# Layer 0's phase table built by GpSimd instead of VectorE, and the last input product of the state space in another PSUM bank

## The reference, cut to what matters

```
h = rmsnorm(x, norm_mix[l])
u, sq, sk, sv, dq, dk, dv, gate_logits = jnp.split(h @ w_in[l], split_idx, axis=-1)
y_ssm = jax.nn.gelu(s5_ssm(u, ...))            # the state space
y_sb  = stick_breaking_attention(sq, sk, sv)
o     = differential_attention(dq_r, dk_r, dv, lam)
...
lam_bar = jnp.exp(lam * dt)                    # in s5_ssm: one complex number for each of 2048 states
bu = jnp.einsum('gpc,blgc->blgp', b_bar, ug)
_, states = lax.associative_scan(_ssm_combine, (a, bu), axis=1)
```

## Time and profile before

| what | value |
|---|---|
| time, median of 3 runs | 1025.34 us (1024.87 to 1025.78) |
| time of the profiled execution | 1024.67 us |
| its span from the first to the last instruction | 1023.0 us |
| granted TensorE clock, mean | 0.997 of full speed |
| PE busy / DVE busy / ACT busy / POOL busy | 96% / 75% / 54% / 5% |

### The profile page before, as it was taken

How to read it: one execution, slowest core, us unless ns; L and a number is a source line. 1 busy time by engine, 2 the same in 40 slices (tenths; PEclk the granted TensorE clock), 3 DMA queues, 4 the chain that set the end, 5 groups by cost and what they waited for, 6 DMA issues and landing times. The chain is left out here.

```text
span 1023.0 us, 17644 instructions
## 1 busy us (share of the span) xinstructions
PE 985.5 (96%) x6784; PEld 872.3 (85%) x6784; DVE 764.5 (75%) x1185; ACT 549.9 (54%) x843; POOL 47.3 (5%) x104
## 2 busy tenths in 40 slices
PE   6999999999999999999999999999999999999996
PEld 6877889999897888888889778999988878888885
DVE  5988997878765866879765669887887567656665
ACT  7455426475755645544463663545656565444543
POOL 5004000000000004000000110000000000000000
PEclk9999999999999999999999999999999999999999
DMA  9797438466654666686657853565565546666652
GB/s 339 230 191 179 125 103 268 147 168 184 181 148 124 244 189 183 190 228 187 191 145 206 169 156 104 151 196 152 179 182 168 141 128 188 194 191 188 186 187 80
DMA packets 64164, 181.37 MB, mean 177 GB/s; under 512 B 19729, under 2 KB 21777, under 8 KB 63441
## 3 DMA queue, kind: packets, MB, share of 16 engines
q1 hardware_dynamic: 63648, 179.91, 60.3%
q10 hardware_dynamic: 432, 0.32, 0.1%
HBM read 176.67 MB, written 3.54 MB: 176 GB/s over the span
## 5 line engine op out<-in xcount | busy, mean ns | idle before, releaser
L1289 DVE TENSOR_TENSOR s_w_lo<-s_raw,s_w_hi 128x1024 fp32r<-128x1024 f32 x312 | 374.1, 1227 | 95.6 <-ACT s_w_hi L914 92.0
L914 ACT ACTIVATE s_w_hi<-s_raw 128x1024 fp32r<-128x1024 f32 x312 | 320.1, 1054 | 180.2 <-PE p_T L1877 78.2
L1875 PE MATMUL p_T<-s_hT,s_w_hi 128*128 128x256 f32 x576 | 166.4, 289 | 1.5 <-ACT s_w_hi L914 1.5
L1876 PE MATMUL p_T<-s_hT,s_w_hi 128*128 128x256 f32 x576 | 163.4, 284 | 0.0
L1877 PE MATMUL p_T<-s_hT,s_w_lo 128*128 128x256 f32 x576 | 163.2, 283 | 0.0
L1875 PE MATMUL p_A<-s_w_hi,s_bT_hi 128*128 128x512 f32 x320 | 125.1, 391 | 2.5 <-DVE s_bT_lo L1289 2.5
L1877 PE MATMUL p_A<-s_w_hi,s_bT_lo 128*128 128x512 f32 x320 | 124.8, 390 | 0.0
L1876 PE MATMUL p_A<-s_w_lo,s_bT_hi 128*128 128x512 f32 x320 | 124.6, 389 | 0.0
L1875 PEld LDWEIGHTS p_T<-s_hT,s_w_hi 128*128 128x128 f32 x576 | 110.8, 192 | 5.5 <-issue 2.7
L1876 PEld LDWEIGHTS p_T<-s_hT,s_w_hi 128*128 128x128 f32 x576 | 110.9, 193 | 0.1
L1877 PEld LDWEIGHTS p_T<-s_hT,s_w_lo 128*128 128x128 f32 x576 | 110.9, 192 | 0.0
(11 more groups left out here) (269 smaller groups left out, 1826.6 us busy)
## 6 DMA issues: line engine op xcount, KB each, us to landing
s_raw<-in_weights SPq DMA_DIRECT2D x312, 512.0 KB, 3.7
s_bt<-in_ssm_bt SPq DMA_DIRECT2D x2, 1024.0 KB, 7.4
s_gates<-f_turn SPq DMA_DIRECT2D x16, 128.0 KB, 7.6
s_x<-in_x SPq DMA_DIRECT2D x1, 1024.0 KB, 10.1
s_dv<-in_ssm_bc SPq DMA_DIRECT2D x2, 512.0 KB, 8.9
u_turn<-s_st_y SPq DMA_DIRECT2D x4, 256.0 KB, 4.9
s_uB<-u_turn SPq DMA_DIRECT2D x16, 64.0 KB, 5.1
s_bt<-in_mem SPq DMA_DIRECT2D x1, 1024.0 KB, 7.1
```

What stands on the lines that cost most here:

```text
L914: return nc.scalar.activation(o, i, f, **kw)
L1289: return V.tensor_tensor(o, i0, i1, op)
L1875: mm(o, lhi, rhi, start=first, stop=False, **kw)
L1876: mm(o, lhi, rlo, start=False, stop=False, **kw)
```

## The change

Two independent edits.

1. In layer 0 the phase table is made by POOL, all six steps in one go (`phases`), right after `tables`. The memsets and the 24 elementwise instructions are the same; the scratch is `dN[1]`, the buffer that dk will be evacuated to, so ACT's evacuation of dk waits for `phase_ready`. On DVE the calls of `p_ph` in layer 0 are gone. Layer 1's table stays on DVE.
2. `ssm_in` part 3 goes to bank A3 in place of A1, in both layers.

```diff
-                    ph=((6, 2, 2), (6, 3, 2), (7, 4, 2), (8, 5, 0), (9, 5, 1)), bt=(10, 11, 12)))
-        after(0, "p_ph0")
+                    bt=(10, 11, 12)))
...
-        [["A1", "A0", "A1", "A1"][s[1]]] if s[0] == "ssm_in" else
+        [["A1", "A0", "A1", "A3"][s[1]]] if s[0] == "ssm_in" else
...
+            def phases(st):
+
+                pool.wait_ge(*st.at(cs_ready, 1))
+                nc.gpsimd.memset(phase[:, 0, :, 0:1], 1.0).then_inc(*st.mid())
+                nc.gpsimd.memset(phase[:, 1, :, 0:1], 0.0).then_inc(*st.mid())
+                for k in range(TAB_STEPS):
+                    pool.wait_ge(*st.mine())
+                    c, e, o, q = phase_step(k, dN[1].rearrange("p t n -> p (t n)"))
+                    tt(o, e, c[0]).then_inc(*st.mid())
+                    tt(q, e, c[1]).then_inc(*st.mid())
+                    pool.wait_ge(*st.mine())
+                    tt(o[:, 0], o[:, 0], q[:, 1], ALU.subtract).then_inc(*st.mid())
+                    tt(o[:, 1], o[:, 1], q[:, 0], ALU.add).then_inc(*(st.sig(phase_ready) if k + 1 == TAB_STEPS else st.mid()))
...
                 if l == 0:
                     tables(st, 0)
+                    phases(st)
...
+                        if kind == "dk":
+                            act.wait_ge(*st.at(phase_ready, 1))
...
-                    elif kind == "p_ph0":
-                        for k in range(2):
-                            p_ph(0, k)
-                            dve.wait_ge(*st.mine())
```

More of the change, by code:

```diff
@@ L170, in pre @@
             after(u["bt"][n], "p_bt", tgt, n)
-        for at, k, part in u["ph"]:
-            after(at, "p_ph", tgt, k, part)
+        for at, k in u.get("ph", ()):
+            after(at, "p_ph", tgt, k)
     if l == 0:
         pre(0, dict(ct=-1, f=(2, 3), cv=(3, 4), b0=5,
-                    ph=((6, 2, 2), (6, 3, 2), (7, 4, 2), (8, 5, 0), (9, 5, 1)), bt=(10, 11, 12)))
-        after(0, "p_ph0")
+                    bt=(10, 11, 12)))
         after(6, "mm_k", 0)
@@ L185, in side_stages @@
         pre(1, dict(ct=up0 + 9, f=(up0 + 13, up0 + 13), cv=(up0 + 12, up0 + 13), b0=up0 + 16,
-                    ph=((up0 + 17, 0, 2), (up0 + 17, 1, 2), (up0 + 17, 2, 2), (up0 + 17, 3, 2),
-                                              (up0 + 20, 4, 2), (up0 + 21, 5, 2)), bt=(up0 + 24, up0 + 25, up0 + 28)))
+                    ph=((up0 + 17, 0), (up0 + 17, 1), (up0 + 17, 2), (up0 + 17, 3), (up0 + 20, 4), (up0 + 21, 5)),
+                    bt=(up0 + 24, up0 + 25, up0 + 28)))
     else:
@@ L468, in hybrid_trunk, with phase_step @@
         e_b = [gates[:, 2 * h:2 * h + 2, :] for h in range(XA_HEADS)]
+        def phase_step(k, scratch):
+            n = 1 << k
+            c = [TURN[:, r, 1 + k, :].unsqueeze(1).unsqueeze(3).broadcast_to([P, 2, STILES, n]) for r in range(2)]
+            q = scratch[:, 0:2 * STILES * n].rearrange("p (r i n) -> p r i n", r=2, n=n)
+            return c, phase[:, :, :, 0:n], phase[:, :, :, n:2 * n], q
         def merged(cb):
@@ L1481, in p_bt, with p_ph @@
                         tt(bT[:, 1], bF[:, 0], bF[:, 1], ALU.add).then_inc(*st.sig(bt_ready))
-                def p_ph(t, k, part=2):
+                def p_ph(t, k):
                     if k == 0:
@@ L1489, in p_ph @@
                         dve.wait_ge(*st.mine())
[L1490 to L1501, removed]
-                        dve.wait_ge(*st.mine())
-                    if part:
-                        tt(o[:, 0], o[:, 0], q[:, 1], ALU.subtract).then_inc(*st.mid())
-                        tt(o[:, 1], o[:, 1], q[:, 0], ALU.add).then_inc(*(st.sig(phase_ready) if k + 1 == TAB_STEPS else st.mid()))
+                    c, e, o, q = phase_step(k, st_y[:, :, :].rearrange("p r n -> p (r n)"))
+                    tt(o, e, c[0]).then_inc(*st.mid())
+                    tt(q, e, c[1]).then_inc(*st.mid())
+                    dve.wait_ge(*st.mine())
+                    tt(o[:, 0], o[:, 0], q[:, 1], ALU.subtract).then_inc(*st.mid())
+                    tt(o[:, 1], o[:, 1], q[:, 0], ALU.add).then_inc(*(st.sig(phase_ready) if k + 1 == TAB_STEPS else st.mid()))
                 def ssm_in(kb):
```

## The result

The changed kernel took 1034.87 us (median of 4 runs, 1034.26 to 1035.45); the kernel before took 1025.12 us (4 runs, 1024.87 to 1025.78). The ratio is 1.0094, 95% interval 1.0081 to 1.0106: slower by 9.7 us. Of the 4.5 us between the two differences of medians 3.0 come from the changed kernel and 1.5 from the kernel before. The times of one kernel differ by up to 3 us with the granted clock, and a good part of this text is about that.

A forecast was written before the change was run, and what follows sets the result against it. PE was taken as the bound over the whole span, following DVE's closed chain from unit 0 to 6. The terms 6.8 + 0.5 + 1.0 - 0 = +8.3 us on 1025.34 gave 1033.6; range 1026.8 to 1038.0.

The forecast's parts named there:

- the blocking: Units 3 to 6: POOL's SBUF reads block DVE's two-SBUF-input instructions, 4112 elements x 2.0 ns = 8.2 us.
- The removal: Steps 0 and 1 leave DVE's list before chunk 6: its chain starts 1.74 us earlier, PE's 1.53 us wait goes.
- The walk: Count along DVE's chain from 27.43, one POOL instruction between two DVE instructions reading SBUF twice: 4112 elements block.
- The clock after the long wait: After PE's wait of some 8 us in unit 6 the clock falls, costing 0.5 us; bounds 0 and 1.7.
- 7.3 forecast for both: Up to `mm_k`: its start 6.8 us later, plus 0.5 us for the lower clock.
- The bank: Layer 0, part 3 in A3: wait moves from `da_t` 0 to `da_t` 1; with a clock fall, net +1.0 us.
- That costs the 1.7 us again: Layer 0: the new 2.9 us wait before `da_t` 1 takes the clock down, costing 1.7 us.
- The premise: Layer 0: PE's 2.02 us wait before `da_t` 0 takes the clock down, so a 2.9 us wait will too.
- The rival in which the bank is worth its whole wait: Layer 0: 2.0 + 1.7 + 1.0 = 4.7 us come off, giving 1027.7; chance 0.06.
- Layer 1: The 0.98 us wait before part 3 goes but moves to `da_t` 0 at 647.82: gain 0.
- POOL's later users: dk's evacuation at 90.65 and the first rotation at 78.13: new wait and longer POOL queue cost nothing.

The follow-up runs named there:

- the second: The same changed kernel measured again on another occasion against the kernel before: 1031.88 us against 1026.64, ratio 1.0063.
- pieces of 128: Layer 0's phase table on POOL, instructions cut to at most 128 elements, bank as before, against the kernel before: 1028.25 us, ratio 1.0023.
- the late kernel: Layer 0's phase table on POOL, started only after `p_b0`, bank as before, against the kernel before: 1027.73 us, ratio 1.0029.
- the faster version: The kernel before with steps 0 and 1 of layer 0's table moved on DVE from unit 0 to unit 6: 1024.33 us, ratio 0.9988.

## Why the prediction was right, and where its sizes were off

The forecast was +8.3 us, 1033.6; the first measurement gave +9.7, 1034.87, the second +5.2 (6.5 by the ratio). Both have the forecast sign, and 1031.9 and 1034.9 lie in the range. The sign and the main term, the blocking, were right with their mechanism; that the sum came out this near is in part luck, since three of its terms were off in both directions. By the steps:

- **The removal, -1.74.** Shown: PE's wait before chunk 6 is gone in every kernel without the steps in unit 0, and the kernel that moves them to unit 6 is 1.2 to 1.5 us faster. What reaches the evacuation of sk is less: the offset there is -1.59 in one trace and -1.03 and -0.95 in two others, in which DVE also starts 0.36 and 0.50 us late and then waits for PE.
- **The blocking, 8.2.** The mechanism is shown: with POOL's reads (fills do nothing), where DVE reads SBUF twice and not where it evacuates PSUM (0.69 kept), in proportion to the elements let in (step 5 out: 5.2 us less), one POOL instruction for each turn (pieces of 128: 0.2 us for a `w_lo`). That two SBUF inputs are needed is not shown: the instruction of the earlier trace rows, which takes 0.95 us beside POOL's copy in every trace, reads one tensor in SBUF, and the same line takes 0.17 elsewhere. Row by row, the pairs named above lost 0.27, 1.44, 0.43, 1.72, 2.59 and 0.94 us, 7.4 in all, 7.5 with the earlier ones. The walk had the turns of the two last steps one DVE instruction late, and one of step 3's instructions of 128 elements stands nowhere in it: `w_lo` 12 and 13 met a 1024 and not a 256, and the last 512 fell ahead of sk and not behind it, so all 3072 elements of step 5 were let in, not 2560. The nanoseconds for an element were off the other way: I took 2.0 from instructions of 128 elements and less. While DVE is idle or reads PSUM, POOL's large instructions show less (the late kernel's timeline of POOL):

```profile
59.62 0.41 POOL L813 TENSOR_TENSOR s_phase<-s_phase,s_small 128x128 f32<-128x128 f32 x1
...
70.80 1.92 POOL L813 TENSOR_TENSOR s_gates<-s_phase,s_small 128x1024 f32<-128x1024 f32 x1
```

  (1.92 - 0.41) / 896 = 1.69 ns. The 4112 elements of the walk then give 6.9 us, and the 512 more that were let in most of the rest up to 7.5; step 5's 5.25 us over its 3072 elements is 1.7 ns again. That its removal brought 5.2 us where 2560 elements x 2.0 ns = 5.1 were expected is therefore two errors that cancel. The evacuation of sk came 5.9 us late, not 6.4, and the table ended at 54.3, not near 57. The figure of the Trainium skill's page "GPSIMD Engine Reference", 2.2 ns an element by its table, would have been further off; this chip's trace has 1.7 for these operands.
- **The clock after the long wait, 0.5.** This term was mis-sized. I let the wait of `mm_k` for `p_b0` hide all but 0.5 of a fall of 1.7 us. The fall was some 6 us at 0.50, and `p_b0` came no later than sk (+5.9, since POOL was done by 54.3): PE never waited for it, and DVE waited 2.17 us for PE at 63.86. The offset grows from 5.91 to 7.88, so the clock cost 2.0: some 6 us at half speed are 3.0, less the wait of 0.80 us before `mm_k` that is gone. Phase edit alone, 0.75 and 1.8 in two traces of one kernel.
- **7.3 forecast for both, 7.9 measured** in the trace (6.6 to 7.8 in three others): the delay was 0.5 to 0.9 too high and the clock 1.5 too low, and they cancelled in part.
- **The bank, +1.0.** The wait moved to `da_t` 1 as forecast (2.83 us for 2.9), and the gain of 0.7 is shown where the clock holds. What failed is "That costs the 1.7 us again": the clock was low for some 7 us in the first trace, and the edit cost 2.25 net in the first trace, 1.9 alone, 0.8 on the faster version, and -0.7 where it did not fall. One number stood for something that differs from execution to execution: the traces have -0.7 to +2.3, where the forecast's bounds were -0.7 and +1.0. The premise failed with it, since the 2.0 us wait does not always take the clock down. On the times the term is not borne out: alone (1.0001), on the phase edit (1.0094 against 1.0069, then 1.0063 against 1.0069) and on the faster version (0.9987 against 0.9988) the intervals overlap each time, the first pair only just. (The rival in which the bank is worth its whole wait takes its 4.7 off 7.1; the terms give 6.8 + 0.5 = 7.3.)
- **Layer 1, 0.** Shown: 1.12 us before `da_t` 0 in place of 0.98, offset 10.3 on both sides.
- **POOL's later users, 0.** Shown: no wait of PE or ACT for the table.

What stays open: what decides between the two clocks after one and the same wait. Nothing in the rows ahead of it differs that I could name. The changed kernel was faster than the phase edit alone on the second occasion, by 1.4 us on the medians; the 1.1 us between the profiled pair (spans 1030.1 and 1031.2) is made up of 0.7 of the bank's gain and 0.9 of a shorter low clock after unit 6, less 0.4 of a later evacuation of sk; the last two may be chance.

## What to carry to other kernels

Ask of an instruction given to GpSimd whether it reads SBUF, and what VectorE does meanwhile: beside two-input SBUF work on VectorE each float32 element of a product or sum cost VectorE some 1.7 ns here, a fill cost nothing, and small pieces limit the loss of each turn. Before another engine is asked, look whether the same engine has a place in which its work is hidden; here moving two steps by six units brought what the move to another engine could not. And a difference of 1 to 2 us that hangs on a wait of 2 to 3 us of TensorE may be one of the clock: look at its executions one by one, and do not price it from one trace.

## What the runs showed of the hardware that I had not expected

- After one and the same wait of 2.83 us the granted clock was at 0.50 for some 7 us in one execution and at 1.00 in another; the offsets behind it differ by 2.9 us (+2.25 and -0.69).
- After the wait of 2.0 us one stage earlier it was low for 3.4 us in most traces, for 6.8 in one, and held in two; after waits of 2.17 us (POOL late, at 78.03) and 2.08 us (pieces, at 57.81) it held too. After one of 1.32 us near 520 it fell in three traces of thirteen.
- After the wait of 6.6 to 7.4 us in unit 6 it was at 0.50 in all four traces, but for 3 to 6 us.
- Fills of 1024 elements on GpSimd took 0.95 us with VectorE beside them (37.16) or idle (1.43, at the start of every kernel), and left it at 2.35 us for a pair of `w_lo`.
- After an idle time in two parts (1.39 and 2.08 us, seven microseconds apart, in the kernel with pieces) the clock held.
